# A gate row spread to all partitions through DRAM in place of products with ones

## The chip, the cores and the metric

The kernel runs on one core of a Trainium2 chip. The metric is the device time of one execution in microseconds; three runs of the kernel before took 290.7, 290.88 and 291.0 us. The engines of the core work side by side, each through its own list of instructions, and wait for each other with semaphores: the matmul engine (PE, with its weight load PEld), VectorE (DVE), ScalarE (ACT), GpSimd (POOL) and SyncE (SP), which here issues every DMA.

## What is computed

One layer of a decoder trunk: 512 positions, 1024 channels, float32. A vector c gives shift, scale and gate; the input is normalised and modulated and goes through one wide projection into an attention group and a convolution group; both are normalised, gated, joined and projected again. The gate, 1024 numbers for the whole sequence, multiplies that result before the residual is added.

```python
mod = jax.nn.silu(c) @ w_ada + b_ada
shift, scale, gate = jnp.split(mod, 3, axis=-1)
h = rmsnorm(x, g_norm) * (1.0 + scale[:, None, :]) + shift[:, None, :]
proj = h @ w_in
q, k, v, z_attn, b_g, c_g, h_c, z_conv = jnp.split(proj, splits, axis=-1)
...
y_attn = rmsnorm(y_attn, g_attn_out) * jax.nn.silu(z_attn)
y_conv = short_gated_conv(b_g, c_g, h_c, w_conv)
y_conv = rmsnorm(y_conv, g_conv_out) * jax.nn.silu(z_conv)
y = jnp.concatenate([y_attn, y_conv], axis=-1) @ w_out
x = x + gate[:, None, :] * y
return rmsnorm(x, g_final)
```

## The kernel before

Each weight is split into a high and a low part so that three products of the fast format stand for one in float32: ACT writes the high part (`slot(n)`, L321), POOL the low part (`slot(n)`, L567). The first part (head, up to about 56 us) makes q, k of the first pair of heads, v and the first C. Then 25 units follow (`UNITS`: H, B, Q, K, ZC, ZA, C of the pairs 0 to 3), each of eight blocks of 128 rows, 24 products of 512 columns (`unit`, L983 to L985), and between them, in an order written out by hand for each engine, the attention of each pair p and head half h: `score` (L1090, L1091), `least` (row minimum, L796, DVE), `exponents` (L388, ACT), `normalise` (reciprocal L801 and four multiplications L806, DVE), `transpose_probs` (L1108, PE), `probs_high` (`pt_hi`, L394, ACT), `probs_low` (`pt_lo`, L812, DVE) and `values` (L1116, PE). The convolution of pair p is `conv_taps` (L761, L768, L771) and `conv_out` (L778) on DVE, its square is `square_y(0, p)` on ACT (L411), which POOL adds up (`add_square`, L573). `rope` (L730 to L734) turns q and k; `q_high` (L355) and `q_low` split q. The output projection (`project`) begins near 235 us and needs `yc_hi`, `yc_lo` and the weights of the slots 25 to 32.

Weights arrive over SP's one list of transfers: three buffers `raw`, the load of slot n waits until POOL has split slot n - 3 (`load_raw`). After some loads stand the copies that double q and k, the last blocks of `w_ada`, and at n = 24 the row `gfin`, read to all partitions at once.

The gate: DVE reduces the last four blocks of `w_ada` with c (`mod_half` 8 to 11) and has the gate as `gcol`, 8 numbers in each of 128 partitions (L890, 153.6 us). It is then needed as a row of 1024 in every partition. In the kernel before DVE multiplies the identity by each column (`gdiag`, L894, 8 instructions); PE multiplies a matrix of ones by the 8 diagonals (`gate_rows`, L1126, between `score(2, 1)` and unit B2) into the banks 5 and 6; ACT copies them to `gate` (L480), between `exponents(2, 1)` and `square_y(0, 2)`; and `transpose_probs(2, 0)`, which writes these banks, waits for the copies. The first use is `residual(0)` (L944), at 260.7 us.

PE's order around it:

```python
score(2, 1)
gate_rows()
unit("B2")
unit("Q3")
transpose_probs(2, 0)
unit("K3")
values(2, 0)
```

Of the kernel before, what the change touches and what calls it, by code (L numbers as in the profile page):

```python
# [4 lines left out]
F32 = mybir.dt.float32  # L5
F32R = mybir.dt.float32r
I32 = mybir.dt.int32
ALU = mybir.AluOpType
ACT = mybir.ActivationFunctionType

P = 128
BANK = 512
# [10 lines left out]
C_B, C_GN, C_GA, C_GC, C_WC, C_SIGN, C_INVF, N_PRM = 0, 24, 32, 36, 40, 52, 64, 96  # L23
# [21 lines left out]
def build(nc, x, c, pos, prm_d, ada_d, whead_d, wslots_d, gfin_d, out):  # L45
# [13 lines left out]

    PIECES = [(0, 0, 512, 5), (0, 512, 1024, 6), (1, 0, 512, 7), (1, 512, 1024, 4), (2, 0, 512, 1),  # L60
              (2, 512, 1024, 0), (3, 0, 512, 2), (3, 512, 768, 3), (3, 768, 1024, 5)]

    with ExitStack() as ctx:
        cursor = [(nc.sbuf_base + 31) // 32 * 32]
# [9 lines left out]
        def sb(name, shape, dt=F32):  # L74
            size = 4
            for n in shape:
                size *= n
            return at(name, room(size), shape, dt)

        def sem(name):  # L80
            return ctx.enter_context(nc.semaphore(name))
# [54 lines left out]
        base = cursor[0]  # L136
        gate = sb("gate", [D])
        mod_junk = at("mod_junk", base, [D])
        gdiag = sb("gdiag", [KT, P])
        base = cursor[0]  # L140
        gfin = sb("gfin", [D])
        c_bc = at("c_bc", base, [D])
# [14 lines left out]
        def bank(b, lo=0, hi=BANK, p0=0, p1=P):  # L157
            return ps[p0:p1, b * BANK + lo:b * BANK + hi]
# [29 lines left out]
        ssq_out, ssq_ok, rs_ok, diag_ok, bc_out = (sem("ssq_out"), sem("ssq_ok"), sem("rs_ok"), sem("diag_ok"),  # L188
                                                   sem("bc_out"))
        y_norm, y_hi, y_lo = sem("y_norm"), sem("y_hi"), sem("y_lo")  # L190
        gcol_ok, gdiag_ok, gate_bc, gate_ok = sem("gcol_ok"), sem("gdiag_ok"), sem("gate_bc"), sem("gate_ok")
        acc_out, om_ok, x2_ok, x2_sq, x2_g = sem("acc_out"), sem("om_ok"), sem("x2_ok"), sem("x2_sq"), sem("x2_g")
        fin_sum, fin_rs, fin_left, fin_right = sem("fin_sum"), sem("fin_rs"), sem("fin_left"), sem("fin_right")

# [30 lines left out]
        @block.sync  # L225
        def _(sp):
            def load_raw(r, src, wide):
                dst, arrived, _ = raw_place(r)
                if 3 <= r < KT + 3:
                    sp.wait_ge(hw_lo, r - 2)  # L230
                elif r >= KT + 3:
                    sp.wait_ge(s_lo, r - KT - 2)
                sp.dma_start(dst[:, 0:wide], src).then_inc(arrived, 16)

            def load_ada(j):
                dst, arrived, _ = ada_place(j)
                if j >= 4:
                    sp.wait_ge(mod_step, 2 * ((j - 4 if j < 10 else j - 2) + 1))
                sp.dma_start(dst[:, :, :], ada_d[j]).then_inc(arrived, 16)

            sp.dma_start(crow[0:1, :], c).then_inc(c_in, 16)
            sp.dma_start(posi[:, :], pos).then_inc(pos_in, 16)
            sp.dma_start(prm[:, :], prm_d).then_inc(prm_in, 16)
            for m in range(TT):
                sp.dma_start(xt[:, m, :], x[m * P:(m + 1) * P, :]).then_inc(x_in[m], 16)
                if m % 2:
                    sp.dma_start(ada[0][:, m // 2, :], ada_d[0, :, m // 2, :]).then_inc(a0_in[m // 2], 16)
            for j in range(KT):
                load_raw(j, whead_d[j], HEAD_W)
                if j + 1 < KT:  # L250
                    load_ada(j + 1)
            def other_rows(dst, src, h, done):

                for a in (0, 64):
                    to, of = a + 32 * (1 - h), a + 32 * h
                    sp.dma_start(dst[to:to + 32, h, :].bitcast(F32), src[of:of + 32, :].bitcast(F32)).then_inc(done, 16)

            def double_q(p):
                sp.wait_ge(q_split, 2 * p + 2)
                sp.wait_ge(qk_lo, 3 * p + 1)  # L260
                for h in range(2):
                    other_rows(qs, q_lo, h, dup_q)

            def double_k(p):
                sp.wait_ge(qk_lo, 3 * p + 3)
                for kd in (kd_hi, kd_lo):
                    for h in range(2):
                        other_rows(kd, kd[:, h, :], h, dup_k)

            for n in range(NSLOT):  # L270
                load_raw(KT + n, wslots_d[n], D)
                if n in (5, 10, 16, 21):
                    double_q((5, 10, 16, 21).index(n))
                if n in (5, 10, 17, 22):
                    double_k((5, 10, 17, 22).index(n))
                if n in (2, 3, 14, 15):
                    load_ada({2: 8, 3: 9, 14: 10, 15: 11}[n])
                if n == NU - 1:
                    sp.wait_ge(mod_step, 2 * NADA)
                    sp.dma_start(gfin[:, :], gfin_d.partition_broadcast(P)).then_inc(gfin_in, 16)  # L280
            sp.wait_ge(scores, 3 * 2 * NP)
            for m in range(TT):
                sp.dma_start(x2[:, m, :], x[m * P:(m + 1) * P, :]).then_inc(x2_in[m], 16)
            for m in range(TT):
                sp.wait_ge(fin_left, m + 1)
                sp.wait_ge(fin_right, m + 1)
                sp.dma_start(out[m * P:(m + 1) * P, :], x2[:, m, :]).then_inc(out_done, 16)
            sp.wait_ge(out_done, 16 * TT)
# [3 lines left out]
        def _(act):  # L292
# [182 lines left out]
            exponents(2, 0)  # L475
            slot(17)
            exponents(2, 1)
            for i in range(2):
                act.wait_ge(gate_bc, i + 1)
                nc.scalar.activation(gate[:, i * BANK:(i + 1) * BANK], bank(5 + i), ACT.Copy).then_inc(gate_ok, 1)  # L480
            square_y(0, 2)
            slot(18)
            q_high(3)
# [142 lines left out]
        def _(dve):  # L626
# [206 lines left out]
            def y_scaled(g, p):  # L833
# [55 lines left out]
            dve.wait_ge(mod_step, 2 * NADA)  # L889
            nc.vector.tensor_tensor(gcol[:, :], acc[:, KT:, :].rearrange("p a b -> p (a b)"),  # L890
                                    prm[:, C_B + 2 * KT:C_B + 3 * KT], ALU.add).then_inc(gcol_ok, 1)
            dve.wait_ge(gcol_ok, 1)
            for i in range(KT):
                ins = nc.vector.tensor_scalar(gdiag[:, i, :], ident[:, :], gcol[:, i:i + 1], None, ALU.mult)  # L894
            ins.then_inc(gdiag_ok, 1)

            least(2, 0)
            conv_taps(2)
# [35 lines left out]
            def residual(e):  # L934
                m, lo, hi, b = PIECES[e]
                dve.wait_ge(acc_out, e + 1)
                if e == 0:
                    dve.wait_ge(gate_ok, 2)
                if e < 2 * TT and e % 2 == 0:
                    dve.wait_ge(x2_in[m], 16)  # L940
                if e >= 2:
                    dve.wait_ge(x2_ok, e - 1)
                o = om[:, e % 2, 0:hi - lo]
                nc.vector.tensor_tensor(o, bank(b, 0, hi - lo), gate[:, lo:hi], ALU.mult).then_inc(om_ok, 1)  # L944
                dve.wait_ge(om_ok, e + 1)
                nc.vector.tensor_tensor(x2[:, m, lo:hi], x2[:, m, lo:hi], o, ALU.add).then_inc(x2_ok, 1)  # L946
# [34 lines left out]
        def _(pe):  # L981
# [113 lines left out]
            def transpose_probs(p, h):  # L1095
                pe.wait_ge(p_norm, 2 * p + h + 1)
                if p == 0 and h == 0:
                    pe.wait_ge(v_lo, TT)
                    pe.wait_ge(c_copy, 1)
                elif h == 0:  # L1100
                    pe.wait_ge(p_lo, 2 * p)
                    if p == 2:
                        pe.wait_ge(gate_ok, 2)
                for i in range(TT):
                    for j in range(i + 1):
                        a = S_AT[i] + j * P
                        o = TB + T_AT[j] + (i - j) * P
                        ins = nc.tensor.transpose(ps[:, o:o + P], probs[h][:, a:a + P], ident[:, :])  # L1108
                ins.then_inc(p_tr, 1)

            def values(p, h):
# [5 lines left out]
                                               pt[:, T_AT[j]:T_AT[j] + S - j * P],  # L1117
                                               start=(j == 0 and n == 0), stop=(j == TT - 1 and n == 1))
                ins.then_inc(pv_out, 1)

            def gate_rows():
                pe.wait_ge(gdiag_ok, 1)
                pe.wait_ge(p_lo, 4)
                for i in range(2):
                    for j in range(4):
                        ins = nc.tensor.matmul(bank(5 + i, j * P, (j + 1) * P), ones[:, :], gdiag[:, 4 * i + j, :],  # L1126
                                               start=True, stop=True)
                    ins.then_inc(gate_bc, 1)

            def y_squares(g):  # L1130
                b = (4, 3)[g]
# [58 lines left out]
            score(2, 0)  # L1190
            unit("H2")
            score(2, 1)
            gate_rows()
            unit("B2")
            unit("Q3")
            transpose_probs(2, 0)
# [53 lines left out]
def host_layout(v):  # L1250
# [12 lines left out]
    def columns(a):  # L1263
        return np.ascontiguousarray(a.reshape(-1, P).T)

    ada = np.empty((12, P, 2, D), np.float32)
    for j in range(12):
        for two in range(2):
            at = (1 - two) * D + j * P if j < 8 else 2 * D + (2 * (j - 8) + two) * P
            ada[j, :, two] = w_ada[:, at:at + P].T  # L1270
    head = np.concatenate([cols("Q0"), cols("K0"), np.arange(start["V"], start["V"] + A), cols("C0")])
    whead = np.ascontiguousarray(w_in[:, head].reshape(8, P, HEAD_W))
    slots = [w_in[:, cols(name)].reshape(8, P, P).transpose(1, 0, 2).reshape(P, D) for name in UNITS]
# [1 line left out]
    slots += [v["w_out"][p * P:(p + 1) * P] for p in range(4)]  # L1275
    prm = np.zeros((P, N_PRM), np.float32)
    prm[:, C_B:C_B + 24] = columns(v["b_ada"])
    prm[:, C_GN:C_GN + 8] = columns(v["g_norm"])
    prm[:, C_GA:C_GA + 4] = columns(v["g_attn_out"])
    prm[:, C_GC:C_GC + 4] = columns(v["g_conv_out"])  # L1280
# [25 lines left out]
```

## Time and profile before

| | us |
|---|---|
| median of three runs | 290.88 |
| the profiled execution | 290.17 |
| its span | 288.1 |
| PE busy | 269.2 (93%) |
| DVE busy | 198.9 (69%) |
| ACT busy | 141.5 (49%) |
| POOL busy | 113.5 (39%) |
| share of the chain that ended last on PE | 82% |
| granted clock of PE, mean of the span | 0.993 |

The span is the time from the first to the last instruction of the trace; the profiled execution's own time has 2.07 us around it. Busy time says who works most, the chain says whose work sets the end: it is followed back from the last instruction, at each step to what released it.

### The profile page before, as it was taken

How to read it: one execution, taken by the hardware profiler on the slowest of the kernel's cores; microseconds unless marked ns; L12 is line 12 of the kernel's file. 1: busy time of each engine (PE TensorE's matmuls, PEld its weight loads, DVE VectorE, ACT ScalarE, POOL GpSimd, SP SyncE). 2: the span in 40 equal slices, each digit the busy share in tenths (PEclk: the TensorE clock that was granted, in tenths of full speed). 3: DMA queues.
4: the chain of work that ended last, by engine and by line, in shares of the span. 5: the costliest groups of instructions: out<-in, count | busy, mean ns of one | idle time of the engine just before them, and what ended most of it. 6: DMA issues, size and time to landing. Idle time of an engine off the chain costs nothing.

```text
span 288.1 us, 3732 instructions
## 1 busy us (share of the span) xinstructions
PE 269.2 (93%) x1300; PEld 223.8 (78%) x1300; DVE 198.9 (69%) x348; ACT 141.5 (49%) x239; POOL 113.5 (39%) x72
## 2 busy tenths in 40 slices
PE   5479999999999999999999999999999979999990
PEld 1358888888888888888888887888888858888880
DVE  4798888699989976788998947623945621304564
ACT  5755355349058833764535254647367574302332
POOL 2400002444534433290461352055086799902321
PEclk9999999999999999999999999999999999999997
DMA  5999944394712462076352203253232518100113
GB/s 192 395 419 417 392 162 146 117 404 126 210 59 73 118 197 88 0 269 243 110 146 74 75 1 102 91 137 144 76 106 78 205 50 305 61 0 2 74 73 146
DMA packets 12260, 43.81 MB, mean 152 GB/s; under 512 B 2129, under 2 KB 2129, under 8 KB 10834
## 3 DMA queue, kind: packets, MB, share of 16 engines
q1 hardware_dynamic: 12242, 43.58, 42.6%
q8 instruction: 10, 0.16, 0.2%
q14 instruction: 8, 0.07, 0.1%
HBM read 38.33 MB, written 2.10 MB: 140 GB/s over the span
## 4 chain that ended last, share of the span: by engine, by line
PE 82%; DMA 4%; ACT 4%; POOL 3%; issue 3%; DVE 2%; SPq 1%; POOLq 0%; ACTq 0%; DVEq 0%
PE ps L983 19%; PE ps L985 18%; PE ps L984 18%; PE ps L1032 5%; DMA xt<-in_x 3%; PE ps L1116 3%; PE ps L1108 2%; PE ps L1045 2%; PE ps L1051 2%; PE ps L1043 2%; PE ps L1091 2%; PE ps L1090 2%; POOL yc_lo L583 2%; PE ps L1049 2%; PE ps L1009 1%
## 5 line engine op out<-in xcount | busy, mean ns | idle before, releaser
L567 POOL TENSOR_TENSOR w_lo<-raw,w_hi 128x1024 fp32r<-128x1024 f32 x29 | 73.7, 2549 | 124.9 <-ACT w_hi L321 124.9
L983 PE MATMUL ps<-h_lo,w_hi 128*128 128x512 f32 x200 | 78.9, 395 | 0.0
L985 PE MATMUL ps<-h_hi,w_hi 128*128 128x512 f32 x200 | 78.0, 390 | 0.0
L984 PE MATMUL ps<-h_hi,w_lo 128*128 128x512 f32 x200 | 77.9, 389 | 0.0
L985 PEld LDWEIGHTS ps<-h_hi,w_hi 128*128 128x128 f32 x200 | 37.6, 188 | 8.0
L984 PEld LDWEIGHTS ps<-h_hi,w_lo 128*128 128x128 f32 x200 | 37.6, 188 | 7.2
L983 PEld LDWEIGHTS ps<-h_lo,w_hi 128*128 128x128 f32 x200 | 37.6, 188 | 7.2
L671 DVE CUSTOM_DVE_ANT_0 mod_junk<-ada,c_bc 128x1024 f32<-128x1024 f32 x22 | 33.4, 1519 | 1.5 <-DVE acc L671 0.6
L388 ACT ACTIVATE probs<-probs,rmin 128x384 f32<-128x384 f32 (+3 forms) x32 | 17.6, 552 | 31.5 <-DVE rmin L796 31.4
L321 ACT ACTIVATE w_hi<-raw 128x1024 fp32r<-128x1024 f32 x29 | 30.1, 1050 | 4.1 <-DMA raw<-in_wslots 4.1
L806 DVE TENSOR_SCALAR probs<-probs,prec 128x384 f32<-128x384 f32 (+3 forms) x32 | 21.4, 733 | 0.3
L944 DVE TENSOR_TENSOR om<-ps,gate 128x512 f32<-128x512 f32 (+1 forms) x9 | 5.7, 629 | 20.7 <-PE ps L985 20.7
L529 ACT ACTIVATE sq_junk<-x 128x512 f32<-128x512 f32 (+1 forms) x9 | 5.3, 585 | 27.5 <-DVE x L946 27.5
L796 DVE CUSTOM_DVE_ANT_0 probs<-mask,ps 128x384 f32<-128x384 f32 (+3 forms) x32 | 13.7, 484 | 4.5 <-PE ps L1091 4.5
L343 ACT ACTIVATE h<-ps,sh,gs 128x512 f32<-128x512 f32 x8 | 6.2, 779 | 20.6 <-DVE sh L680 20.0
L983 PE MATMUL ps<-w_lo,yc_hi 128*128 128x512 f32 (+1 forms) x36 | 13.8, 382 | 1.9 <-POOL yc_lo L583 1.9
L812 DVE TENSOR_TENSOR pt_lo<-ps,pt_hi 128x1280 fp32r<-128x1280 f32 x8 | 11.9, 1487 | 4.1 <-ACT pt_hi L394 4.1
L394 ACT ACTIVATE pt_hi<-ps 128x1280 fp32r<-128x1280 f32 x8 | 9.9, 1238 | 8.3 <-PE ps L1108 8.3
L985 PE MATMUL ps<-w_hi,yc_hi 128*128 128x512 f32 (+1 forms) x36 | 13.3, 371 | 0.0
L984 PE MATMUL ps<-w_hi,yc_lo 128*128 128x512 f32 (+1 forms) x36 | 13.3, 370 | 0.0
L985 PE MATMUL ps<-wa_hi,ya_hi 128*128 128x512 f32 (+1 forms) x36 | 13.2, 367 | 0.0
L984 PE MATMUL ps<-wa_hi,ya_lo 128*128 128x512 f32 (+1 forms) x36 | 13.2, 366 | 0.0
(150 smaller groups left out, 508.5 us busy)
## 6 DMA issues: line engine op xcount, KB each, us to landing
raw<-in_wslots SPq DMA_DIRECT2D x33, 512.0 KB, 3.3
ada<-in_ada SPq DMA_DIRECT2D x11, 1024.0 KB, 9.1
raw<-in_whead SPq DMA_DIRECT2D x8, 448.0 KB, 7.2
xt<-in_x SPq DMA_DIRECT2D x4, 512.0 KB, 5.6
x<-in_x SPq DMA_DIRECT2D x4, 512.0 KB, 6.9
out<-x SPq DMA_DIRECT2D x4, 512.0 KB, 2.7
ada<-in_ada SPq DMA_DIRECT2D x2, 512.0 KB, 7.3
qs<-q_lo SPq DMA_DIRECT2D x16, 64.0 KB, 2.0
```

Of the source, the lines that this page charges most:

```text
L321: nc.scalar.activation(slot_place(n)[0], src[:, :], ACT.Copy).then_inc(s_hi, 1)
L388: nc.scalar.activation(probs[h][:, a:a + w], probs[h][:, a:a + w], ACT.Exp, scale=-1.0, bias=rmin[:, e:e + 1], accum_out=psums[:, e:e + 1] ...
L394: nc.scalar.activation(pt_hi[:, :], ps[:, TB:TB + TRI], ACT.Copy).then_inc(p_hi, 1)
L567: nc.gpsimd.tensor_tensor(lo, src[:, :], hi.bitcast(F32), ALU.subtract).then_inc(s_lo, 1)
L671: dve.tensor_tensor_reduce(mod_junk[:, :], src[:, two, :], c_rows, 1.0, 0.0, ALU.mult, ALU.add, acc[:, j, two:two + 1]).then_inc(mod_step, 1)
L796: dve.tensor_tensor_reduce(probs[h][:, a:a + w], mask[:, S - w:S], ps[:, SB + a:SB + a + w], 1.0, 3.0e38, ALU.add, ALU.min, rmin[:, e:e + ...
L806: ins = nc.vector.tensor_scalar(probs[h][:, a:a + w], probs[h][:, a:a + w], prec[:, e:e + 1], None, ALU.mult)
L812: nc.vector.tensor_tensor(pt_lo[:, :], ps[:, TB:TB + TRI], pt_hi[:, :].bitcast(F32), ALU.subtract).then_inc(p_lo, 1)
L983: nc.tensor.matmul(o, a_hi, b_lo, start=start, stop=False)
L984: nc.tensor.matmul(o, a_lo, b_hi, start=False, stop=False)
L985: return nc.tensor.matmul(o, a_hi, b_hi, start=False, stop=stop)
L1032: nc.tensor.matmul(o, a_hi, b_hi, start=(j == 0), stop=False)
```

## The change

`gcol` is written to a DRAM tensor of 128 times 8 numbers, and read back as one row of 1024 to all 128 partitions. So that this row has the right order, the host gives the columns of `w_ada` and of the bias so that partition p holds the gate's channels 8p to 8p + 7 (before: channels p, 128 + p, and so on). The write is issued by SP behind the load of slot 20, the read behind that of slot 24 and ahead of `gfin`. `gdiag`, its eight multiplications, the eight products, the two copies and the wait of `transpose_probs(2, 0)` go; `residual(0)` waits for the read.

```diff
+    gate_d = nc.dram_tensor("gate_row", [P, KT], F32, kind="Internal").ap()
...
-        gdiag = sb("gdiag", [KT, P])
...
+                if n == 20:
+                    sp.wait_ge(gcol_ok, 1)
+                    sp.dma_start(gate_d, gcol[:, :]).then_inc(gate_out, 16)
                 if n == NU - 1:
+                    sp.wait_ge(gate_out, 16)
+                    sp.dma_start(gate[:, :], gate_d.rearrange("p k -> (p k)").partition_broadcast(P)).then_inc(gate_in, 16)
                     sp.wait_ge(mod_step, 2 * NADA)
                     sp.dma_start(gfin[:, :], gfin_d.partition_broadcast(P)).then_inc(gfin_in, 16)
...
             exponents(2, 1)
-            for i in range(2):
-                act.wait_ge(gate_bc, i + 1)
-                nc.scalar.activation(gate[:, i * BANK:(i + 1) * BANK], bank(5 + i), ACT.Copy).then_inc(gate_ok, 1)
             square_y(0, 2)
...
-            dve.wait_ge(gcol_ok, 1)
-            for i in range(KT):
-                ins = nc.vector.tensor_scalar(gdiag[:, i, :], ident[:, :], gcol[:, i:i + 1], None, ALU.mult)
-            ins.then_inc(gdiag_ok, 1)
...
-                    dve.wait_ge(gate_ok, 2)
+                    dve.wait_ge(gate_in, 16)
...
                     pe.wait_ge(p_lo, 2 * p)
-                    if p == 2:
-                        pe.wait_ge(gate_ok, 2)
...
-            def gate_rows():
-                pe.wait_ge(gdiag_ok, 1)
-                pe.wait_ge(p_lo, 4)
-                for i in range(2):
-                    for j in range(4):
-                        ins = nc.tensor.matmul(bank(5 + i, j * P, (j + 1) * P), ones[:, :], gdiag[:, 4 * i + j, :],
-                                               start=True, stop=True)
-                    ins.then_inc(gate_bc, 1)
...
             score(2, 1)
-            gate_rows()
             unit("B2")
...
-            at = (1 - two) * D + j * P if j < 8 else 2 * D + (2 * (j - 8) + two) * P
-            ada[j, :, two] = w_ada[:, at:at + P].T
+            at = (1 - two) * D + j * P
+
+            of = slice(at, at + P) if j < 8 else slice(2 * D + 2 * (j - 8) + two, None, 8)
+            ada[j, :, two] = w_ada[:, of].T
...
+    prm[:, C_B + 16:C_B + 24] = v["b_ada"][2 * D:].reshape(P, 8)
```

## Rows read from the trace of the kernel before

**Rows 1.** The page, chain that ended last: shares of the span by engine.

```profile
PE 82%; DMA 4%; ACT 4%; POOL 3%; issue 3%; DVE 2%; SPq 1%; POOLq 0%; ACTq 0%; DVEq 0%
```

**Rows 2.** Timeline of PE, 158.6 to 161.4: start, us, engine, line, operation, count.

```profile
159.26 1.95 PE L1126 MATMUL ps<-gdiag,ones 128*128 128x128 f32 x16
160.96 0.47 PE L983 MATMUL ps<-h_lo,w_hi 128*128 128x512 f32 x1
```

**Rows 3.** The chain that ended last, in order of time: start, us, what.

```profile
159.42 1.78 PE ps L1126 x16
...
172.17 0.69 DVE m L730
...
177.34 1.50 DVE pt_lo L812
178.88 1.49 PE ps L1116 x8
...
214.30 1.17 PE ps L1108 x10
...
230.36 5.02 POOL yc_lo L583 x4
```

**Rows 4.** Waits of PE from 140 us: who waited for whom, us, times, longest.

```profile
PE ps L983 <- POOL yc_lo L583: 1.9, 4, 1.0
PE ps L1116 <- DVE pt_lo L812: 0.2, 1, 0.2
```

**Rows 5.** Timeline of DVE, 153 to 173 (in brackets: idle before, released by).

```profile
153.81 1.66 DVE L894 TENSOR_SCALAR gdiag<-ident,gcol 128x128 f32<-128x128 f32 x8
...
158.97 0.49 DVE L768 TENSOR_SCALAR yc<-u,prm 128x512 f32<-128x512 f32 x1
159.50 3.62 DVE L771 SCALAR_TENSOR_TENSOR yc<-u,prm,yc 128x512 f32<-128x512 f32 x2
...
164.42 0.55 DVE L796 CUSTOM_DVE_ANT_0 probs<-mask,ps 128x384 f32<-128x384 f32 x1
...
167.61 1.27 DVE L806 TENSOR_SCALAR probs<-probs,prec 128x384 f32<-128x384 f32 x4
172.17 0.69 DVE L730 TENSOR_TENSOR m<-ps,cos_t 128x512 f32<-128x512 f32 x1 [3.28 <-PE ps L985]
```

**Rows 6.** Timeline of ACT, 158 to 169.

```profile
158.30 1.04 ACT L321 ACTIVATE w_hi<-raw 128x1024 fp32r<-128x1024 f32 x1
...
167.21 1.06 ACT L480 ACTIVATE gate<-ps 128x512 f32<-128x512 f32 x2
168.17 0.63 ACT L411 ACTIVATE sq<-yc 128x512 f32<-128x512 f32 x1
```

**Rows 7.** Timeline of POOL, 159 to 173: all that it runs there.

```profile
159.42 2.36 POOL L567 TENSOR_TENSOR w_lo<-raw,w_hi 128x1024 fp32r<-128x1024 f32 x1 [6.94 <-ACT w_hi L321]
168.87 1.30 POOL L573 TENSOR_TENSOR sqsum<-sqsum,sq 128x512 f32<-128x512 f32 x1 [7.09 <-ACT sq L411]
170.12 2.39 POOL L567 TENSOR_TENSOR w_lo<-raw,w_hi 128x1024 fp32r<-128x1024 f32 x1
```

**Rows 8.** DVE at 112; DVE by shape at 124.5 (busy, mean ns); POOL at 124.

```profile
112.75 1.54 DVE L771 SCALAR_TENSOR_TENSOR yc<-u,prm,yc 128x512 f32<-128x512 f32 x2
...
L806 DVE TENSOR_SCALAR probs<-probs,prec 128x128 f32<-128x128 f32 x1 | 2.4, 2420 | 0.0
...
124.23 2.52 POOL L567 TENSOR_TENSOR w_lo<-raw,w_hi 128x1024 fp32r<-128x1024 f32 x1
```

**Rows 9.** DMA issues (KB, us to landing); timelines of SP and ACT after 200.

```profile
raw<-in_wslots SPq DMA_DIRECT2D x33, 512.0 KB, 3.3
gfin<-in_gfin SPq DMA_DIRECT2D x1, 512.0 KB, 4.1
...
202.35 35.96 SPq L233 DMA_DIRECT2D raw<-in_wslots  x8
...
217.79 1.99 ACT L321 ACTIVATE w_hi<-raw 128x1024 fp32r<-128x1024 f32 x2
```

More of the change, by code:

```diff
@@ L190, in build @@
         y_norm, y_hi, y_lo = sem("y_norm"), sem("y_hi"), sem("y_lo")
-        gcol_ok, gdiag_ok, gate_bc, gate_ok = sem("gcol_ok"), sem("gdiag_ok"), sem("gate_bc"), sem("gate_ok")
+        gcol_ok, gate_out, gate_in = sem("gcol_ok"), sem("gate_out"), sem("gate_in")
         acc_out, om_ok, x2_ok, x2_sq, x2_g = sem("acc_out"), sem("om_ok"), sem("x2_ok"), sem("x2_sq"), sem("x2_g")
```

## The prediction

> **What bounds the kernel now.** I read the page first. Its chain that ended last is 82% matmul engine (PE) [rows 1], so a microsecond counts where PE has to run or to wait, and elsewhere only if it makes PE wait. Next the PE timeline around the block that goes: the passes of `gate_rows` begin at 159.26 us, 0.12 us behind the start of the last score product, and the first product of unit B2 begins at 160.96 [rows 2]. PE stands nowhere in between. The chain in order of time gives the same block 1.78 us for 16 passes [rows 3]. Then PE's own waits from 140 us on: only 1.9 us before the first output products (four short waits for `yc_lo`) and 0.2 us in `values(2, 0)`, for `pt_lo` [rows 4]. So from `gate_rows` to about 230 us PE is full, and the only place where another engine is level with it is that 0.2 us. The chain around it shows why: Q3 ends on PE, then come rope on DVE from 172.17, the q split and `pt_hi` on ACT, `pt_lo` on DVE from 177.34 with 1.50, and PE goes on at 178.88 [rows 3]. This path has no slack at all behind the start of rope(Q3): what delays rope delays PE by the same amount.
>
> **What goes from PE.** Eight products, seen as 16 passes, 1.78 us on the path. Nothing takes their place: B2's weights (slot 15) were split before 150, and the bank that B2 writes was read by `copy_c(2)` before 152.1, so B2 can begin 1.78 us earlier. The wait of `transpose_probs(2, 0)` for `gate_ok` ended at about 168.3 with the copies of 167.21 [rows 6], over 3 us before PE came to it; it was worth nothing. Term one: -1.78 us.
>
> **What goes from DVE.** Eight multiplications into `gdiag`, 1.66 us from 153.81 [rows 5], plus the step to them, so `least(2, 0)` can begin at 153.8 in place of 155.5. It is not on PE's path; but it sets when ACT reaches slot 17 (158.30, [rows 6]) and so when POOL splits it (159.42, [rows 7]). Both come some 1.78 us earlier: POOL's split of slot 17 will run from about 157.64 to 160.0. Unit H2, for which `conv_taps(2)` waits, does not move, for it stands ahead of `gate_rows`.
>
> **What goes from ACT.** Two copies out of PSUM, 1.06 us from 167.21 [rows 6]. ACT idled over 5 us before the q split at 175.02, so by itself this is worth nothing. But it brings `square_y(0, 2)` and slot 18 close behind the exponents, and with them POOL's sum and slot 18. That is where I expect part of the gain to be given back.
>
> **What the earlier POOL does to DVE.** The trace shows an L806 multiplication of 128x128 that took 2.42 us [rows 8] where the four of `normalise` together take 1.27 when nothing is beside them [rows 5]. POOL ran a split from 124.23 for 2.52 us: the DVE instruction stood until POOL's had ended. At the seam between two POOL instructions one waiting DVE instruction got through. The L771 pair at 159.50 (3.62 us in place of the 1.54 that such a pair takes with POOL idle) stood in the same way under the split of 159.42 [rows 5, 7, 8]; the products that read PSUM (rope, `pt_lo`) show no such stretch.
> The Trainium skill, SBUF — State Buffer, section "SBUF: two separate sides", says that VectorE and GpSimd share a port pair under an exclusive lock, held for the whole instruction, and that the other fully blocks. The trace agrees (2.42 us of blocking). Taken as if there were no such lock, the sum would be the full -1.78 us, my first rival.
>
> Now the order of events with the change, step by step:
> - POOL splits slot 17 until 160.0. The first tap (L768, at 158.97 as now) stands until then and ends near 160.27; the two L771 then run free, 1.54 us with a seam of 0.1 to what follows [rows 8]. The next step, the reciprocal, comes near 161.76 in place of 163.03. So `least(2, 1)` begins at about 163.15 in place of 164.42 [rows 5]: 1.27 us earlier, not 1.78.
> - Exponents(2, 1) hang on it: from 164.42 to the next ACT instruction at 167.21 are 2.79 us [rows 5, 6]. Call that end E: now 167.21, then 165.94.
> - Now the two gate copies stand between E and the square (168.17), POOL's sum begins at 168.87, and the four multiplications of `normalise(2, 1)` (167.61 plus 1.27 = 168.88) just get out ahead of it [rows 5 to 7]. With the change the square begins at E, POOL's sum 0.70 later at E + 0.70, and slot 18 follows at E + 1.95, to end at about E + 4.41. The multiplications begin at E + 0.40 as now. The first is under way when POOL begins; the second stands until E + 2.0, the third until E + 4.41 plus 0.19 to its successor, the last leaves DVE free at about E + 4.86 = 170.80.
> - Q3 ends on PE at 172.14 - 1.78 = 170.36, and rope could begin at 170.39. It begins at 170.80. Term two: +0.41 us, and it arrives at PE in full, as the wait of `values(2, 0)` for `pt_lo`: 0.17 now, about 0.6 then.
> Bounds of term two: at the low end 0, if the second multiplication slips in before POOL (they come within some 0.03 us of each other) and the rest ends near 170.3. At the high end E does not move at all: 167.21 + 4.86 - 170.39 = 1.68. I take the middle reckoning, 0.41, since each of its steps copies a row.
>
> **What is added.** The write of `gcol` goes to SP's queue behind the load of slot 20, which waits for slot 17 (about 160.0); `gcol_ok` is met at 153.8, so SP doesn't stand. One issue of some 0.43 us; the next load waits for slot 18, ten microseconds on. The trace has no DMA of 32 bytes per partition to DRAM. Nearest rows: the loads of 512 KB at 3.3 and of `gfin` at 4.1 us [rows 9]. I take 2 to 4 us, and it has until 198 us: cost 0, from below too, as no transfer is made earlier by it. The Trainium skill, DMA: Bandwidth & Descriptors, section "Specifications", says that transfers under 512 bytes are done by read-modify-write; no row here shows it for a store, and the sum would be the same by it.
> The read back has the shape and the size of `gfin`, 512 KB, 4.1 us to land [rows 9]. It stands at n = 24, ahead of `gfin`. Behind it are `gfin` (used at 263) and the load of slot 25, issued at 202.35; with 3.3 us it lands at 205.7, and ACT takes it at 217.79 [rows 9]. One more transfer of 512 KB pushes it back by at most 4.1 us; 12 us of slack hide that. Cost 0; without this cover it would be up to 4.1. The gate is used at 260.7, 60 us after. `residual(0)` waits for `gate_in` in place of `gate_ok`, both long done. The shorter SBUF plan and the new order of the host's columns move no instruction.
>
> **Does the rest follow?** After `values(2, 0)` all engines hang on PE again. The last wait of PE (1.9 us) ends a chain that starts from PE's own transposes at 214.30 and goes through ACT, POOL and a load to `yc_lo` at 230.36 [rows 3]; it moves with PE and neither eats nor returns the gain.
>
> **Sum.** -1.78 + 0.41 = -1.37 us. For the profiled execution: 290.17 - 1.37 = 288.80, span 288.1 - 1.37 = 286.7. The median of the runs, 290.88, lies 0.71 above that execution; I take the difference over: 290.88 - 1.37 = 289.5.
>
> **The rivals.**
> - *All of it stays.* DVE is free when Q3 ends: 290.88 - 1.78 = 289.1. For it: the second multiplication and POOL's sum come within hundredths, and an E only 0.4 us earlier does the same. Against it: the stalls of [rows 8]. Chance 0.28.
> - *My forecast,* term two between 0.1 and 0.9: 289.2 to 290.0. Chance 0.55.
> - *Nothing measurable.* If the split of slot 17 does not come earlier (a slower start of the exponents) and DVE loses there what `gdiag` gave, E stays near 167.2 and rope is 1.2 to 1.7 us late: 290.3 to 290.8. The same figure would come if PE had another wait behind `gate_rows`, so that the change doesn't take off the path what it takes off PE; the waits of PE speak against that [rows 4]. Chance 0.12.
> - *Slower.* SP stands at n = 24 until the write of 128 small pieces has landed. Up to about 202 that is free; then slot 25's load is late, free for 12 more. ACT takes slot 25 at 217.8, by then 216.4; less 3.3 for its load and 0.9 for two issues, the write must have landed by 212.2, some 52 us after its issue at 160.4. Only beyond that is ACT's split held up, and with it PE one for one; at 53.4 us the gain is eaten, at 56 the time is 289.5 + 4 = 293.5. Nothing in the rows takes a quarter of that. Chance 0.05.
>
> **How the numbers follow.** The likeliest case gives 289.5. A measurement of this kernel can tell about 0.2%, 0.58 us, from no change; the first two cases lie beyond that: faster 0.83, within 0.12, slower 0.05. The range takes in the first case and a part of the third, and 0.2 us for the runs' own spread (290.7 to 291.0): 288.9 to 290.2.
>
> **What would show it.** PE: the last score product of (2, 1) followed by B2 with 0.12 us between. POOL: the sum of `sqsum` beginning at about 166.6 and slot 18 ending at 170.3. DVE: L806 of (2, 1) taking over 3 us in place of 1.27, and no idle time before rope(Q3). PE's wait for `pt_lo` at 0.5 to 0.7 us in place of 0.2. The wait for `yc_lo` unchanged at 1.9. SP: no wait at `gate_out`. The prediction is wrong if DVE idles before rope(Q3) (then 289.1), or if PE waits anywhere else between 160 and 230.

## The result

The changed kernel takes 288.82 us (median of four runs, 288.66 to 289.36) against 290.94 for the kernel before; the ratio is 0.9929, with a 95% interval of 0.991 to 0.9947. That is 2.1 us less, 0.1 us below the range of the prediction. Two later comparisons of the same two kernels gave 0.9951 (0.992 to 0.9982) and 0.9933 (0.9908 to 0.9958), 1.4 and 1.9 us. The change is a gain; its size is known to some 0.5 us from these medians alone.

The traced execution of the changed kernel took 289.36 us with a span of 287.6, only 0.5 us shorter than the span before. The reason is at the very start. The page's chain and the waits of PE over the whole span, changed kernel (columns as in [rows 4]):

```profile
PE 77%; DVE 6%; ACT 4%; DMA 4%; POOL 3%; issue 3%; SPq 1%; POOLq 0%; ACTq 0%; DVEq 0%
```

```profile
PE ps L1008 <- DVE xt L688: 2.0, 1, 2.0
PE ps L982 <- POOL yc_lo L586: 1.9, 4, 1.0
...
PE ps L1113 <- DVE pt_lo L815: 0.7, 1, 0.7
```

PE waited 2.0 us for the normalised x, where the trace of before shows 1.3: the load of x that stands in both chains took 8.53 us in place of 7.81. The wait for `yc_lo` is 1.9 as in [rows 4]; the one for `pt_lo` has grown from 0.2 to 0.7. And DVE has gone from 2% of the chain [rows 1] to 6%, though no more work was given to it.

To keep the start out, all traces here are compared over one stretch: from the start of the last product of `score(2, 1)`, just ahead of the change, to the start of DVE's last instruction. Before: 159.14 to 284.27, **125.13 us**. Changed: 159.79 to 283.68, **123.89 us**. PE's timeline at the beginning of it, which answers [rows 2]:

```profile
159.79 0.28 PE L1090 MATMUL ps<-kd_hi,qs 128*128 128x256 f32 x1
159.90 0.40 PE L982 MATMUL ps<-h_lo,w_hi 128*128 128x512 f32 x1
```

B2 begins 0.11 us behind the score product, with nothing between. Now DVE, against [rows 5]:

```profile
154.46 0.56 DVE L799 CUSTOM_DVE_ANT_0 probs<-mask,ps 128x384 f32<-128x384 f32 x1
...
159.62 1.43 DVE L771 TENSOR_SCALAR yc<-u,prm 128x512 f32<-128x512 f32 x1
161.09 1.54 DVE L774 SCALAR_TENSOR_TENSOR yc<-u,prm,yc 128x512 f32<-128x512 f32 x2
...
163.94 0.55 DVE L799 CUSTOM_DVE_ANT_0 probs<-mask,ps 128x384 f32<-128x384 f32 x1
...
167.07 4.54 DVE L809 TENSOR_SCALAR probs<-probs,prec 128x384 f32<-128x384 f32 x4
171.53 0.68 DVE L733 TENSOR_TENSOR m<-ps,cos_t 128x512 f32<-128x512 f32 x1
```

and POOL, against [rows 7]:

```profile
158.37 2.40 POOL L570 TENSOR_TENSOR w_lo<-raw,w_hi 128x1024 fp32r<-128x1024 f32 x1 [5.24 <-ACT w_hi L327]
167.43 1.29 POOL L576 TENSOR_TENSOR sqsum<-sqsum,sq 128x512 f32<-128x512 f32 x1 [6.66 <-ACT sq L417]
168.68 2.39 POOL L570 TENSOR_TENSOR w_lo<-raw,w_hi 128x1024 fp32r<-128x1024 f32 x1
```

The four multiplications of `normalise(2, 1)` take 4.54 us in place of 1.27, and `rope("Q3")` starts straight behind them: DVE's 3.28 us of idle time are gone. By shape (busy, mean ns of one), in the stretch from 167 us:

```profile
L809 DVE TENSOR_SCALAR probs<-probs,prec 128x512 f32<-128x512 f32 x1 | 2.6, 2627 | 0.0
L809 DVE TENSOR_SCALAR probs<-probs,prec 128x128 f32<-128x128 f32 x1 | 1.4, 1396 | 0.0
...
L809 DVE TENSOR_SCALAR probs<-probs,prec 128x384 f32<-128x384 f32 x1 | 0.4, 420 | 0.0
L809 DVE TENSOR_SCALAR probs<-probs,prec 128x256 f32<-128x256 f32 x1 | 0.3, 341 | 0.0
```

The first (384) was under way; the second (128) stood until POOL's sum ended and got through at the seam between the sum and the split; the third (512) stood through the whole split; the fourth (256) ran free. The transfers are in SP's list and among the landings:

```profile
161.17 1.05 SPq L281 DMA_DIRECT2D gate_row<-gcol  x1
...
197.54 0.43 SPq L284 DMA_DIRECT2D gate<-gate_row  x1
```

```profile
gate<-gate_row SPq DMA_DIRECT2D x1, 512.0 KB, 5.4
gfin<-in_gfin SPq DMA_DIRECT2D x1, 512.0 KB, 6.2
gate_row<-gcol SPq DMA_DIRECT2D x1, 4.0 KB, 3.3
```

The write of 128 pieces of 32 bytes lands in 3.3 us, the read back in 5.4, and `gfin` behind it in 6.2 in place of 4.1 [rows 9].

### The profile page after: what moved, and what is told of

It reads as the page before. It is cut to its first block, busy times and chain, and to the rows that moved or that the text cites. A ratio compares the mean times of both kernels' runs of the same rounds, so it can differ in the third digit from the quotient of the medians.

```text
span 287.6 us, 3691 instructions
## 1 busy us (share of the span) xinstructions
PE 267.3 (93%) x1284; PEld 221.5 (77%) x1284; DVE 199.7 (69%) x340; ACT 140.6 (49%) x237; POOL 114.2 (40%) x72
## 4 chain that ended last, share of the span: by engine, by line
PE 77%; DVE 6%; ACT 4%; DMA 4%; POOL 3%; issue 3%; SPq 1%; POOLq 0%; ACTq 0%; DVEq 0%
PE ps L982 17%; PE ps L984 17%; PE ps L983 17%; PE ps L1031 5%; DMA xt<-in_x 3%; PE ps L1113 3%; PE ps L1105 2%; PE ps L1044 2%; PE ps L1050 2%; DVE probs L809 2%; POOL yc_lo L586 2%; PE ps L1042 2%; PE ps L1048 2%; PE ps L1090 2%; PE ps L1089 2%
## 5 line engine op out<-in xcount | busy, mean ns | idle before, releaser
L809 DVE TENSOR_SCALAR probs<-probs,prec 128x384 f32<-128x384 f32 (+3 forms) x32 | 24.7, 834 | 0.3
```

The source lines that it names most:

```text
L809: ins = nc.vector.tensor_scalar(probs[h][:, a:a + w], probs[h][:, a:a + w], prec[:, e:e + 1], None, ALU.mult)
```

## The experiments

Theory L (on record before the result): taking the copies off ACT lets POOL begin its sum and split while `normalise(2, 1)` is under way; they block DVE; rope(Q3) is late, and PE pays. Theory R: there is no such coupling; what is missing of PE's 1.78 us is paid elsewhere, and the copies, the transfers and gdiag's time count each by itself or not at all.

### The two kernels again

> The kernel before, once more, to learn what its own runs and heads do. Three readings of why the measured gain (2.1 us) is larger than the 1.2 us that the two spans show once the later start of the first block in the trace of after (PE's wait for x, 2.0 against 1.3 us) is taken out. (A) The first loads land up to 0.7 us sooner or later from run to run, whatever the kernel: then this kernel's spans lie anywhere between 288.1 and 288.9, and its trace shows a wait of PE for x that accounts for it. (B) The kernel before has a second loss in most of its runs that its one trace did not catch: then spans near 288.9 with a head as early as in the trace of before, and a longer wait or product later on. (C) The runs of before simply lie by chance 0.3 to 0.5 high: ratio 1.000 within 0.1%, and the median here near 290.5.

> The changed kernel, once more. The theory that was forecast (POOL holds the multiplications of normalise(2,1) and rope(Q3) starts late): ratio 0.9929 to 0.9958, and in the trace L809 of 167 us takes 4.0 to 4.8 us, PE waits 0.6 to 0.8 for pt_lo. The rival (in most runs the second multiplication slips in before POOL and the traced run was an exception): L809 near 1.3 to 3.0 us, PE waits 0.2, ratio 0.9939.

Before: ratio 1.0005 (0.9983 to 1.0028), stretch 159.94 to 285.30, 125.36 us, PE waits 1.8 us for x and 0.2 for `pt_lo`. Changed: ratio 0.9951, stretch 160.21 to 284.06, 123.85 us; the multiplications take 4.54 us again and PE waits 0.7. So the blocked multiplications were no exception of one trace. Reading A holds for the spread only in part: spans of before lie between 287.9 and 289.8 at a mean granted clock of 0.992 to 0.994, more than the 288.1 to 288.9 expected, and of the 0.8 us by which this trace's stretch starts later than the first one's, PE's wait for x has 0.5. There is a second part to the spread, beyond what was expected: runs with a mean granted clock of 0.987 to 0.989, which are 1 to 2.3 us longer on the mean. "At full clock" below means without those. And a third: the time around the span is 2.03 us on average for before (1.95 to 2.09) and 1.80 for the changed kernel (1.75 to 1.83).

### ACT's two copies put back

```diff
             exponents(2, 1)
+            for i in range(2):
+                nc.scalar.activation(gate[:, i * BANK:(i + 1) * BANK], mask[:, :], ACT.Copy)
             square_y(0, 2)
```

> The changed kernel with two copies of 128x512 put back on ScalarE where the gate's copies stood (mask to the gate's buffer, which the transfer overwrites later), without any wait: 1.06 us more work on ScalarE. The theory that the early sum on GpSimd blocks DVE: the multiplications of normalise(2,1) are out before GpSimd begins (1.3 us in place of 4.5), rope(Q3) starts on time, PE's wait for pt_lo falls from 0.7 to 0.2, and the kernel is 0.5 us faster than the changed one, ratio to before 0.9911 to 0.992. The rival (rope is late for another reason, or ScalarE's time counts by itself): the same as the changed kernel or slower by up to 1 us.

DVE's timeline and POOL's:

```profile
165.96 1.27 DVE L811 TENSOR_SCALAR probs<-probs,prec 128x384 f32<-128x384 f32 x4
169.89 0.69 DVE L735 TENSOR_TENSOR m<-ps,cos_t 128x512 f32<-128x512 f32 x1 [2.65 <-PE ps L986]
```

```profile
167.36 1.30 POOL L578 TENSOR_TENSOR sqsum<-sqsum,sq 128x512 f32<-128x512 f32 x1 [7.69 <-ACT sq L417]
```

With more work on ACT the multiplications take 1.27 us and are out at 167.23, 0.13 us ahead of POOL. DVE idles 2.65 us before rope, PE waits 0.2, the stretch is 158.68 to 282.07, **123.39 us**: 0.5 less than the changed kernel, 1.74 less than before, close to PE's 1.78. At full clock the median is 288.46, as against 289.10. The ratio over all its runs is 0.9952 (0.9926 to 0.9978), short of what was expected, since eight of its twelve runs had the low granted clock; why it met so many is open.

### gdiag's multiplications put back, alone and with the copies

```diff
             nc.vector.tensor_tensor(gcol[:, :], ...).then_inc(gcol_ok, 1)
+            dve.wait_ge(gcol_ok, 1)
+            for i in range(KT):
+                nc.vector.tensor_scalar(gdiag[:, i, :], ident[:, :], gcol[:, i:i + 1], None, ALU.mult)
 
             least(2, 0)
```

> The changed kernel with the eight multiplications into gdiag put back on DVE, with no reader: 1.66 us more work on DVE, far from PE's path. The theory: everything behind comes 1.3 us later on DVE while Q3 still ends early, so the exponents (2,1) end where they did before the change, GpSimd's two instructions hold the multiplications until about 1.6 us after Q3's end; PE waits 1.6 to 1.9 us for pt_lo, and nearly the whole gain is gone: 1.0 to 1.2 us slower than the changed kernel, ratio 0.997 to 0.9995. The rival (DVE has slack there, its 3.3 us of idle time before Q3 hides the work): the same time as the changed kernel.

Alone:

```profile
159.07 3.63 DVE L775 SCALAR_TENSOR_TENSOR yc<-u,prm,yc 128x512 f32<-128x512 f32 x2
...
167.14 4.54 DVE L810 TENSOR_SCALAR probs<-probs,prec 128x384 f32<-128x384 f32 x4
171.60 0.68 DVE L734 TENSOR_TENSOR m<-ps,cos_t 128x512 f32<-128x512 f32 x1
```

PE's wait (us in total, times, longest):

```profile
PE ps L1117 <- DVE pt_lo L816: 1.8, 1, 1.8
```

The tap pair is blocked as in the kernel before (3.63 us, [rows 5]), and `normalise(2, 1)` then by the sum and the split. 1.66 us of work that has nothing to do with PE costs PE 1.1 us more of waiting, as expected. The time came out worse than expected: the ratio is 1.0005 (0.9986 to 1.0024), eight products off the path and no measurable gain, and at full clock the kernel is 1.6 us slower than the changed one, not 1.0 to 1.2. Some 0.25 us of the difference lie outside the span, as the last experiments show.

> The changed kernel with both the eight multiplications into gdiag and the two copies on ScalarE put back: of the change only PE's products and the transfers are left. The theory: with both, the order of DVE, ScalarE and GpSimd is that of the kernel before, so the multiplications of normalise(2,1) come out ahead of GpSimd as they did, and PE keeps the whole 1.78: stretch of 123.35 us, PE waits 0.2 for pt_lo. The rival (each instruction put back costs by itself): slower than the kernel with gdiag alone, whose PE waited 1.8. Around the span: 2.03 us if the gdiag instructions make the difference from 1.78 that the runs so far show.

Both: the ratio is back at 0.9947 (0.9921 to 0.9973), PE waits 0.2 us, DVE idles 1.50 us before rope. The kernel with more work is faster than the one with less: 288.81 against 290.67 us at full clock. That excludes theory R for these two parts. (Its stretch of 124.81 us contains a fall of the clock, for which see the end.)

### GpSimd held back, by a wait and by an order

```diff
+            pool.wait_ge(p_norm, 6)
             add_square(0, 2)
```

> The changed kernel; GpSimd waits for the multiplications of normalise(2,1) before its sum of the squares (2), nothing else. The theory (GpSimd's sum and split block them): they take 1.3 us, GpSimd begins some 1 us later, rope(Q3) starts when Q3 ends, PE's wait for pt_lo is 0.2, and from the last score product of (2,1) to the last instruction of DVE there are 123.35 us (changed kernel 123.87, before 125.13 and 125.36). The rival (ScalarE's extra time in the run with the copies gave the gain in another way, not through GpSimd): the stretch stays at 123.9. Median among the runs whose granted clock is not low: 288.4 to 288.6, 0.5 under the changed kernel's.

> The version in which GpSimd waits for normalise(2,1), again: 0.5 us under the changed kernel on the same chip, ratio to before 0.990 to 0.9925; stretch of 123.4 us, PE waits 0.2 us for pt_lo.

Ratio 0.9912 (0.9883 to 0.994), stretch 159.33 to 282.76, **123.43 us**, L810 1.28 us, PE waits 0.2; and again 0.9926 (0.9899 to 0.9954), with the same 1.28 and 0.2; this second trace's stretch, 125.16 us, has a fall of the clock in it and misses the 123.4. At full clock the medians are 288.38 and 288.43. The edit touches GpSimd's list alone, so it is GpSimd's place in time that made DVE late.

```diff
             exponents(2, 1)
-            square_y(0, 2)
             slot(18)
+            square_y(0, 2)
```

> The changed kernel with ScalarE's slot 18 ahead of its square of the convolution (2), so that GpSimd's sum, which waits for the square, begins some 1.05 us later; no wait and no instruction is added. The theory: the four multiplications of normalise(2,1) are out before GpSimd begins (1.3 us), PE waits 0.2 us for pt_lo, stretch of 123.4 us, as with the added wait. The rival (the wait on GpSimd helped in some other way): as the changed kernel, 4.5 us, 0.7 us, 123.9.

```profile
166.34 1.28 DVE L809 TENSOR_SCALAR probs<-probs,prec 128x384 f32<-128x384 f32 x4
170.26 0.69 DVE L733 TENSOR_TENSOR m<-ps,cos_t 128x512 f32<-128x512 f32 x1 [2.64 <-PE ps L984]
```

Two lines of ACT's list exchanged do the same without a wait: POOL's sum begins at 167.64, at the end of the multiplications (167.62). Ratio 0.99 (0.9875 to 0.9925), the lowest of all, with an interval that overlaps the others'; PE waits 0.2. Its one trace has a fall of the clock in the stretch (125.16 us), so its times and the rows above speak for it, not the stretch. The changed kernel on the same chip:

> The changed kernel a third time, to be compared on one chip with the two that leave DVE free: median among runs whose granted clock is not low 288.9 to 289.2, 0.5 us above theirs; stretch 123.9 us.

Ratio 0.9933, 288.76 at full clock, L809 4.55 us, PE waits 0.7; 0.3 to 0.5 us above the two that leave DVE free, by the means at full clock (288.77 against 288.48 and 288.26). The stretch of its trace, 125.45, has a fall of the clock too, which was not expected.

### The transfers alone

The kernel before with the write and the read added and used, and the products, gdiag and the copies kept.

```diff
+                if n == 20:
+                    sp.wait_ge(gcol_ok, 1)
+                    sp.dma_start(gate_d, gcol[:, :]).then_inc(gate_out, 16)
                 if n == NU - 1:
+                    sp.wait_ge(gate_out, 16)
+                    sp.dma_start(gate[:, :], gate_d.rearrange("p k -> (p k)").partition_broadcast(P)).then_inc(gate_in, 16)
...
```

> The kernel before with the two transfers added and their result used; the products, gdiag and the copies stay and their result is overwritten. It measures what the transfers cost alone. The theory: nothing, ratio 0.999 to 1.001, stretch of 125.1 to 125.4 us, PE waits 0.2 for pt_lo, the loads of the slots 24 and 25 land long before ScalarE takes them. The rival (the transfers hold something up, and that is what the changed kernel pays in place of the blocked DVE): 0.3 to 0.6 us slower.

Ratio 1.0009 (0.9988 to 1.0029), stretch 159.43 to 284.62, 125.19 us, between the two traces of before (125.13 and 125.36). The transfers cost nothing measurable.

### The time around the span

```diff
         mod_junk = at("mod_junk", base, [D])
+        gdiag = sb("gdiag", [KT, P])
```

> The changed kernel with gdiag's 4 KB per partition kept in the SBUF plan and no instruction that uses it: all addresses are those of the kernel before. It is for the time around the span, 2.03 us in every run of the kernel before and of the one with gdiag's instructions, 1.78 in every run of the changed one. Theory A (addresses or the size of the plan): 2.03 here. Theory B (the eight instructions on DVE): 1.78 here. Within the span: as the changed kernel, stretch 123.9, PE waits 0.7 for pt_lo.

gdiag's room in SBUF without its instructions: 1.81 us around the span (1.77 to 1.84), as the changed kernel; stretch 158.61 to 282.56, 123.95 us; ratio 0.9955 (0.9928 to 0.9983). So addresses are not it.

```diff
+            for i in range(KT):
+                nc.vector.tensor_scalar(rmin[:, i:i + 1], ones[:, i:i + 1], 1.0, None, ALU.mult)
             for e in range(len(PIECES)):
                 residual(e)
```

> The changed kernel with eight multiplications of 128x1 on DVE ahead of the first residual, where DVE has idled for 13 us; no reader. It is for the time around the span: 2.03 us in every run of kernels whose DVE list holds gdiag's eight instructions, 1.76 to 1.81 without. If the number of instructions in DVE's list makes it, 2.03 here; if it is gdiag's place or size, 1.78 here. Within the span no change from the changed kernel (stretch 123.9).

2.03 us around the span (1.98 to 2.08); stretch 160.02 to 283.90, 123.88 us; ratio 0.9925 (0.9903 to 0.9948). Eight tiny instructions on DVE at another place bring the 2.03 back, with no overlap between the runs of either kind. So 0.25 us of the change's gain lies outside the span and comes with eight instructions more or fewer in DVE's list, at both places where they were tried. The length of the other lists did not do it: two more instructions on ACT left 1.79 (copies put back), and PE's sixteen passes fewer left 2.02 (both put back). What makes the difference there, no run shows.

## Why the prediction was wrong

The path inside the span was right, step by step; the sum lacked a term outside it, and more was gained than all terms that the runs show add up to.

| | forecast | measured |
|---|---|---|
| term one, PE's products | -1.78 | -1.74 (125.13 to 123.39, copies put back; -1.84 from the mean of three traces, 125.23) |
| `least(2, 1)` earlier, counted from the last score product, by | 1.27 | 1.13 (5.28 before, 4.15 after) |
| POOL's sum behind the next ACT instruction after the exponents | 0.70 | 0.70 (166.73, 167.43) |
| the multiplications of (2, 1) | over 3 us | 4.54 |
| PE's wait for `pt_lo` | about 0.6 | 0.7 |
| wait for `yc_lo` | 1.9 | 1.9 |
| transfers | 0 | 0 (125.19 against 125.13 and 125.36) |
| the stretch | -1.37 | -1.24 (123.89); -1.34 between the means of four traces (123.89) and three (125.23) |
| gdiag's time outside the span | none | -0.25 |

**Term two was right in kind and in size.** It was reckoned as 0.41 and came out at 0.5. Two of its steps were off by little and in opposite directions: slot 18 ends at E + 4.34 by [rows 6, 7], where it writes 4.41, and `least(2, 1)` moved by 1.13, not 1.27. The order of events that gave it (the stall under the split of slot 17 moves from the tap pair to the first tap; two POOL instructions behind each other; one DVE instruction through the seam) is what the rows of the changed kernel show: the first tap (L771 there, L768 before) at 1.43 in place of 0.49, the pair at its free 1.54. The high end, 1.68, was shown too: with gdiag's time kept, PE waited 1.8 us where it waits 0.2 with DVE free, 1.6 more.
The rule of the Trainium skill (SBUF — State Buffer, "Who interferes with whom") that a DVE instruction with at most one SBUF input outside the two-port modes does not contend with GpSimd, while one with two SBUF inputs does, agrees with two rows of the kernel before: L730, with one of its inputs in PSUM, ran in 0.69 us beside a split (172.17, POOL until 172.51, [rows 5, 7]), and the pair with two SBUF inputs took 3.62 beside one. The multiplications of `normalise` have a single tensor input in SBUF and stood all the same; by this rule they would have to be in a two-port mode, and no trace names the mode.

**The step that failed is the sum's last one.** "The shorter SBUF plan and the new order of the host's columns move no instruction" agrees with the run that keeps gdiag's room (stretch 123.95), but the sum takes span and time down by the same 1.37 (288.1 to 286.7, 290.17 to 288.80), and so puts the change of the 2.07 us around the span at nothing, without a reason. With eight instructions fewer in DVE's list they are about 1.8. With this term the forecast would have been 290.88 - 1.37 - 0.25 = 289.26, inside the range that it gave and still 0.44 above what was measured.

**The remaining 0.4 us to 288.82 stay open.** The prediction saw three runs within 0.3 us and took 0.2 us for the spread. Over all runs of the kernel before the times lie between 289.8 and 292.6 us: the start of the stretch alone lies between 158.61 and 160.21 us among the fourteen traces, and the kernels with the change (158.61 to 160.21) and those with before's order of work (159.14 to 159.94) are mixed in it. The three measured differences, 2.1, 1.4 and 1.9 us, lie around what the traces and the time around the span explain, 1.34 + 0.25 = 1.6. Chance has a part in that, but hardly all of it: over all runs at full clock the kernel before takes 290.83 us (66 runs) and the changed one 288.89 (19 runs), 1.94 us less with a standard error of 0.10. Some 0.3 us of this are in no term that a run shows. The traces do not resolve them: the stretch shows 1.34 us, and three traces of one side are too few for a start that moves by 1.6 us.

**The rivals.** That all of the 1.78 stays did not happen, though its number, 289.1, lies nearer to the measured time than the forecast's: that is luck, for PE waited 0.7 us and DVE did not idle before rope. The third, nothing measurable, is what the kernel with gdiag's time kept does (1.0005). The slower one needed a write of over 50 us; it took 3.3.

## What to carry to other kernels

Work taken from an engine off the path shifts what stands behind it; if that is a GpSimd stretch, look which DVE instructions with SBUF operands it will now fall upon, and whether PE hangs on them. Here the gain of eight products taken off PE was lost by 1.66 us of DVE work far from PE's path (1.0005), and the 0.5 us that the changed kernel had left were brought in by exchanging two lines of another engine's list (0.99). A column of 128 x 8 numbers can be spread to all partitions through DRAM for nothing where tens of microseconds lie between its making and its use, as here: 3.3 us out, 5.4 us back.

## What the runs showed that was not expected

**The clock falls behind waits of PE, in some executions.** The trace with gdiag kept, two stretches (PE busy and count, PEld, DVE, ACT, POOL, then the granted clock, the DMA share, GB/s):

```profile
175.00:179.00 4.00, 2.17 (x10) 1.50 (x9) 2.92 (x4) 2.66 (x4) 1.26 (x1) 1.00 0.17 41
179.00:183.00 4.00, 4.00 (x20) 3.81 (x19) 2.52 (x4) 1.49 (x2) 1.12 (x1) 0.57 0.51 156
```

PE had waited 1.8 us in the first; in the second the granted clock was 0.57 on the mean, so for most of it the lower of the two levels (1.2 GHz). With 1.6 us more waiting than with the copies (123.39) its stretch should be 125.0; it is 126.59, so the fall cost about 1.6. In four other traces the clock fell a few microseconds behind the waits for `yc_lo` (four waits up to 234 us, 1.8 to 2.1 us in all, the longest 0.9 to 1.2); the changed kernel's third:

```profile
232.00:234.00 2.00, 1.61 (x6) 0.68 (x4) 0.59 (x1) 1.37 (x2) 2.00 (x2) 1.00 0.00 0
...
236.00:238.00 2.00, 2.00 (x11) 1.81 (x11) 0.91 (x2) 0.00 (x0) 1.51 (x2) 0.67 0.22 49
238.00:240.00 2.00, 2.00 (x6) 1.52 (x6) 0.00 (x0) 1.23 (x5) 2.00 (x2) 0.50 0.93 354
```

Its stretch is 125.45 against 123.89, 1.56 us. The same waits stand in the other traces without a fall, so it can fall after them and need not. That the waits cause the fall is not shown, since no run took them away; if they do, the 1.9 us at `yc_lo` are worth more than 1.9 to whoever removes them.

**Eight instructions on DVE are 0.25 us outside the span,** both of 128x128 and of 128x1, as told above.
